# Moving weight slots and the shared region off multiples of 2048 bytes in a one-core fp32r encoder block

## What is computed

```python
mods = split(silu(c) @ w_ada + b_ada, 9)        # three times shift, scale, gate
x += 0.5 * g1 * swiglu(modulate(rmsnorm(x, norm_g[0]), sh1, sc1), w_ffn1_in, w_ffn1_out)   # FF = 2816
z  = modulate(rmsnorm(x, norm_g[1]), sh2, sc2) @ w_mix_in      # 3328 columns
x += g2 * concat(hgrn2_group(z...), windowed_gqa(z...)) @ w_mix_out
x += 0.5 * g3 * swiglu(modulate(rmsnorm(x, norm_g[2]), sh3, sc3), w_ffn2_in, w_ffn2_out)
```

## Time and profile before

| | us |
|---|---|
| device time, median of 2 runs | 1063.08 (1061.94 to 1064.22) |
| the profiled execution | 1063.89 |
| its span, first to last instruction | 1062.1 |
| TensorE busy, 5028 matmuls | 1043.2 |
| VectorE busy | 589.4 |
| ScalarE busy | 395.7 |
| GpSimd busy | 49.0 |

### The profile page before, as it was taken

One profiled execution on the slowest core, in us unless ns is written; L12 is line 12 of the kernel. 1 busy time (PEld: TensorE's weight loads), 2 busy tenths in 40 slices (PEclk: granted clock), 3 DMA queues, 4 the chain that ended last, 5 costly groups with the idle time before them and its releaser, 6 DMA issues.

```text
span 1062.1 us, 12566 instructions
## 1 busy us (share of the span) xinstructions
PE 1043.2 (98%) x5028; PEld 862.2 (81%) x5028; DVE 589.4 (55%) x674; ACT 395.7 (37%) x438; POOL 49.0 (5%) x33
## 2 busy tenths in 40 slices
PE   5999999999999999999999999999999999999998
PEld 3888888888888888888888898888888888888887
DVE  5896554554754689467788649873222232333323
ACT  4644242332323255363435773452121212323231
POOL 0000000000000060010200000510000000000000
PEclk9999999999999999999999999999999999999999
DMA  9657645546446422432120031313323223232312
GB/s 349 213 201 277 224 169 200 195 177 219 159 162 233 161 82 80 107 92 80 41 70 30 2 80 41 110 49 119 118 79 109 89 89 109 79 119 79 118 40 79
DMA packets 93738, 133.50 MB, mean 126 GB/s; under 512 B 10721, under 2 KB 77149, under 8 KB 93574
## 3 DMA queue, kind: packets, MB, share of 16 engines
q1 hardware_dynamic: 93374, 130.83, 36.1%
q10 hardware_dynamic: 328, 2.17, 0.5%
HBM read 130.88 MB, written 4.21 MB: 127 GB/s over the span
## 4 chain that ended last, share of the span: by engine, by line
PE 94%; DVE 3%; DMA 1%; ACT 1%; issue 1%; SPq 0%; DVEq 0%; ACTq 0%
PE bank L1745 26%; PE bank L1747 26%; PE bank L1746 26%; PE bank L2071 2%; PE bank L2180 2%; PE bank L2273 1%; PE bank L2166 1%; PE bank L1879 1%; PE bank L1885 1%; PE bank L1893 1%; PE bank L2155 1%; DMA x_nat<-in_x 1%; PE bank L1830 1%; PE bank L2256 1%; DVE tmod L1177 1%
## 5 line engine op out<-in xcount | busy, mean ns | idle before, releaser
L1745 PE MATMUL bank<-h_hi,w_hi 128*128 128x512 f32 x880 | 345.7, 393 | 0.1
L1747 PE MATMUL bank<-h_hi,w_lo 128*128 128x512 f32 x880 | 342.6, 389 | 0.0
L1746 PE MATMUL bank<-h_lo,w_hi 128*128 128x512 f32 x880 | 342.5, 389 | 0.0
L1103 DVE TENSOR_TENSOR w_lo<-w_raw,w_hi 128x2048 fp32r<-128x2048 f32 x81 | 186.5, 2303 | 276.9 <-ACT w_hi L675 276.8
L675 ACT ACTIVATE w_hi<-w_raw 128x2048 fp32r<-128x2048 f32 x81 | 155.2, 1916 | 490.5 <-PE bank L1747 485.3
L1745 PEld LDWEIGHTS bank<-h_hi,w_hi 128*128 128x128 f32 x880 | 165.2, 188 | 36.4 <-issue 2.1
L1747 PEld LDWEIGHTS bank<-h_hi,w_lo 128*128 128x128 f32 x880 | 165.2, 188 | 34.7
L1746 PEld LDWEIGHTS bank<-h_lo,w_hi 128*128 128x128 f32 x880 | 165.3, 188 | 34.1 <-issue 0.5
L1745 PE MATMUL bank<-a_hi,w_hi 128*128 128x512 f32 x352 | 137.6, 391 | 0.0
L1747 PE MATMUL bank<-a_hi,w_lo 128*128 128x512 f32 x352 | 137.0, 389 | 0.0
L1746 PE MATMUL bank<-a_lo,w_hi 128*128 128x512 f32 x352 | 137.0, 389 | 0.0
(11 more groups left out here) (270 smaller groups left out, 953.1 us busy)
## 6 DMA issues: line engine op xcount, KB each, us to landing
w_raw<-in_w_ffn_in SPq DMA_DIRECT2D x42, 1024.0 KB, 4.9
ada<-in_w_ada SPq DMA_DIRECT2D x28, 1024.0 KB, 5.0
w_raw<-in_w_ffn_out SPq DMA_DIRECT2D x22, 1024.0 KB, 4.9
w_raw<-in_w_mix_in SPq DMA_DIRECT2D x11, 1024.0 KB, 5.1
shift_in<-in_w_ada SPq DMA_DIRECT2D x4, 1024.0 KB, 8.3
scale_in<-in_w_ada SPq DMA_DIRECT2D x4, 512.0 KB, 6.8
x_nat<-in_x SPq DMA_DIRECT2D x2, 1024.0 KB, 8.7
scale_half<-in_w_ada SPq DMA_DIRECT2D x2, 1024.0 KB, 10.4
```

What stands on the lines that cost most here:

```text
L1103: ve.tensor_tensor(w_lo[n % 2][:], src[:], as_f32(w_hi[n % 2][:]), ALU.subtract).then_inc(wlo_done, 1)
L1745: te.matmul(out_ap, wh, xh, start=first, stop=False)
L1746: te.matmul(out_ap, wh, xl, start=False, stop=False)
L1747: return te.matmul(out_ap, wl, xh, start=False, stop=last)
```

## The change

Only addresses in SBUF change; the instructions, waits and transfers are the same. `next_to` is `take` without rounding.

```diff
+    def next_to(nbytes):
+        here = top[0]
+        top[0] += nbytes
+        return here
...
+    masks = at("masks", [P, LEVELS, P], mybir.dt.uint8, take(1024))
+    sel_b = at("sel_b", [10, 2, P], f32r, take(1024))
+    st = at("softmax_stats", [P, 5, 32], f32, take(640))
     ident = at("ident", [P, P], f32, take(512))
     ones = at("ones", [P, P], f32, take(512))
...
     O_RAW0, O_RAW1 = take(8 * KB), take(8 * KB)
     raw = [at(f"w_raw{s}", [P, 2048], f32, o) for s, o in enumerate((O_RAW0, O_RAW1))]
-    o_w_hi0, o_w_hi1, o_w_lo0, o_w_lo1 = (take(8 * KB) for _ in range(4))
+    cact = at("cact", [P, DT], f32, take(32))
+    top[0] = O_RAW1 + 8 * KB + 64
+    o_w_hi0, o_w_lo0 = next_to(8 * KB), next_to(8 * KB)
+    ind_qk = at("ind_qk", [P, 18], f32, take(72))
+    sink_r = at("sink_r", [1, QH], f32, take(32))
+    top[0] = o_w_lo0 + 8 * KB + 192
+    o_w_hi1, o_w_lo1 = next_to(8 * KB), next_to(8 * KB)
+    top[0] = (top[0] + 63) // 64 * 64
+    vec = at("vec", [P, P], f32, take(512))
...
     region = take(0)
-    assert XT_AT % 2048 == 0 and region % 2048 == 0
+    region += (32 - region) % 2048
+    assert XT_AT % 2048 == 0
```

More of the change, by code:

```diff
@@ L163, in build @@
     raw = [at(f"w_raw{s}", [P, 2048], f32, o) for s, o in enumerate((O_RAW0, O_RAW1))]
-    o_w_hi0, o_w_hi1, o_w_lo0, o_w_lo1 = (take(8 * KB) for _ in range(4))
+    cact = at("cact", [P, DT], f32, take(32))
[7 more added lines that the diff above has]
+    vec = at("vec", [P, P], f32, take(512))
+    modv = at("modv", [P, 9 * DT], f32, take(288))
+    fac = at("fac", [P, 3, DT], f32, take(96))
+    gates = at("gates", [P, 3, DT], f32, take(96))
+    eps_t = at("eps_t", [P, 1], f32, take(4))
+    ind_r = at("ind_r", [P, 18], f32r, take(72))
+    sink_b = at("sink_b", [P, QH], f32, take(32))
+    neg_sink = at("neg_sink", [P, QH], f32, take(32))
+    qg8 = at("qg8", [P, 1], f32, take(4))
+    relb = at("relb", [NB + 1, QH], f32, take(32))
+    warm = at("warm", [P, 3], f32, take(12))
+    rms0 = at("rms0", [P, 3, TT], f32, take(48))
+    wbias = at("wbias", [P, 2, 2], f32, take(16))
+    wb0 = at("wb0", [P, 4], f32, take(16))
     w_hi = [at(f"w_hi{s}", [P, 2048], f32r, o) for s, o in enumerate((o_w_hi0, o_w_hi1))]
```

## The result

The changed kernel takes 1078.61 us (median of 2 runs, 1077.90 to 1079.32) against 1063.08: the ratio is 1.0146, with a 95% interval of 1.0091 to 1.0201. It is slower by about 15.5 us, beyond the interval, and above the forecast's 1070 us. Two per cent lie just inside the interval.

What follows compares the result with a forecast made beforehand. The prediction took TensorE's fp32r matmul pace to bound the kernel. Its terms, 0 + 0 + 0 + 0.4 = +0.4 us on the median of 1063.1 us, gave 1063.5 us, with a range from 1018 to 1070 us.

Steps and rivals of the forecast that it cites:

- What bounds the kernel, the count and the pace: TensorE, busy 98% at 2.4 GHz throughout: 3,984 fp32r matmuls at 226.7 ns, 903 us, 85% of the span.
- The stake: Main stream: 10.5 ns a matmul between the fp32r pace and the fp32 pace of 216.2 ns, 41.8 us in all.
- Rivals A and B: Main stream: offsets end the 10.5 ns conflict wholly (A, 1021.7 us, chance 0.26) or in part (B, 1032.8 to 1052.4, 0.16).
- the term of TensorE's main stream: The 3,984 fp32r matmuls: address change costed at 0, bounds -41.8 us and +21 us, called the term most open.
- the ten-column loads: Five matmuls at 517.63 us loading 10 weight columns, 230 ns each; taken as evidence against a conflict of reads.
- The second reason for 0: Main stream: it keeps one pace, 226.7 ns, through everything the kernel before varies, so 0 between the bounds.
- Rival C: Main stream: with slots at two offsets it never settles; 232 ns, +21 us, 1084.6 us; chance 0.15.
- The small terms: Small fp32 passes 0 (at most 8.8 us), other engines 0 (at most 4.2), transfers +0.4 us (at most 1.2).

Runs made afterwards that it cites:

- e11_narrow_aligned: Kernel before, with slot 0's stages of the second feed-forward multiplying only 64 or 32 weight columns with h, 16 with a; 1065.94 us (one run).
- e8_low_parts: Everything at a multiple of 256 except `h_lo` and slot 0's `w_lo`, both 64 bytes past one; 1079.22 us (one run).
- e9_all_256: Changed kernel with its three offsets rounded to multiples of 256; 1063.44 us against 1062.97 for the kernel before, ratio 1.0001.
- e1_slots_only: Changed kernel with the region back at a multiple of 2048, so only weight slots move; ratio to the kernel before 1.0133, 14.1 us.

## Why the prediction was wrong

**What bounds the kernel, the count and the pace** were right: 15.2 us are 3,744 matmuls of `three` at a changed pace, and the 240 others of the same shape add about 0.3. The clock was not quite at 2.4 GHz throughout: near 28 us both traces have 3.4 us at a granted clock of 0.50 (1.2 GHz), too short for the 40 slices to show, and the same before and after. **The stake** (10.5 ns a matmul down to the fp32 pace) was not one: none of 22 distances gives back anything of the 13.3 ns. Rivals A and B fall with it.

**The step that failed** is the term of TensorE's main stream, put at 0: "The load of weights does not look like the cause ... If the two reads met in a bank, reading a thirteenth of the weights should have helped. I therefore cost this edit at 0". It measured +15.2 us: 233.3 ns a matmul where the distance isn't 0 by 256. The step reads the ten-column loads as a test of whether weights and stream meet, and they can't be one. They changed two things at once, the width (10 columns) and the start (8 bytes apart, off the multiples of 512 of everything else). `e11_narrow_aligned` shows that the width alone gives their pace: loads of 16 columns at aligned starts run at 231.1 ns, as these did at 230 to 232. So the row spoke neither for nor against an effect of addresses. What it did show was that the stream can stay above 226.7 ns. That fewer bytes do not help was right; that the weights are then not the cause did not follow: with `w_lo` alone moved (`e8_low_parts`, slot 0 with a) the pace is 231.0 ns.

**The second reason for 0**, that "the stream sits at one pace through everything the kernel before varies", was true and empty. All it varied were multiples of 512, all of them a distance of 0 by 256. The text said so itself ("an effect of 32, 64 or 256 bytes has no row") and still took the middle. Where every row sits on one point of a grid, the rows give no reason to put the term at nothing.

**Rival C** had the mechanism and nearly the price: the disturbed pace of the earlier trace rows, 232 ns, as the steady one. Measured are 233.3. C let the whole stream run unsettled, because the slots stand at two offsets. Measured is that each slot and tile kind has its own pace: 48 of 78 stages of `three` are slow, and nearly all of the others are slot 1 with h, at a distance of 256, which settle again after each slow stage. They need about six matmuls for that, 0.7 us over all of them. So the loss is 15.5 us where C said 21. C had a chance of 0.15, and its sum (1084.6) was left outside a range that ended at 1070.

**The small terms** held: the fp32 passes are unchanged; the first wait for `x_nat` is 0.14 us longer. The Trainium skill (DMA: Bandwidth & Descriptors, How a descriptor splits into AXI transactions) speaks of the bytes fetched from where a descriptor starts; if that holds for the end where `x_nat` lands too, which the page doesn't say, the wait is one beat in 129 longer, an estimate of 0.08 us. A single wait in one execution each cannot tell that from chance, and `e9_all_256`, whose transfers start at multiples of 256 again, has the time of the kernel before with or without it.

**What stays open.** Why the stream always finds its way to 226.7 ns at a distance of 0 and only now and then at 16 or 144, and why narrow slices keep it from there, the runs don't show. The prediction's picture of two reads that meet in a bank is neither shown nor excluded by them; they show no waiting instruction, only starts that come later. Nor is it shown that 226.7 ns could not be bettered by something else than addresses. Each swept distance stands in one or two kernels with one execution each; the stages of a kernel repeat it. The 14.1 us of `e1_slots_only` are 1.7 more than its stages give, within its interval.

## What to carry to other kernels

In a stream of fp32r matmuls of 128x128 weights and 512 columns, give the weight slices and the streamed tiles the same remainder by 256 bytes, high and low parts alike; here that is worth up to 6.6 ns of 233.3 in each. Multiples of 2048 are fine but not needed. When a change moves addresses, list which remainders the old trace has tried; where it has tried one only, the trace gives no reason to expect nothing.

## What the runs showed of the hardware

- The same instruction has several steady paces: 226.7 ns a matmul when all operands share their remainder by 256, and mostly 228 to 234 ns else, at a granted clock of 1.00 in both. The slower paces alternate, for instance 236 and 231 ns at a distance of 64, with a pattern that differs by distance.
- Distance is not all: at a distance of 16 one stage of 48 ran at 226.7 ns and the next one of the same slot at 233.3.
- After a break at a distance of 0 the stream takes five to ten matmuls of 224 to 236 ns before it is back at 226.7.
- At a granted clock of 0.50 (near 28 us, slot 0 with h) these matmuls start 426 to 427 ns apart in the kernel before and in the changed one alike. 512 columns at 1.2 GHz are 426.7: neither the 13.3 ns nor the distance of 64 shows there.
- The settled pace was seen with whole slices alone: with 64, 32 or 16 of 128 columns, and all starts aligned, it is 230 to 232 ns.
- An offset of 4 bytes costs 5.6 ns of the possible 6.6, and the curve isn't smooth: 8 bytes 4.1 ns, 240 bytes 1.7, 248 bytes 6.7.
